# Start offsets within 128 bytes of the split weight and activation buffers in a hybrid decoder layer

## The reference, cut to what matters

```python
proj = h @ lp['w_in'] + lp['b_in']                       # D_MODEL 2048 -> 10288 columns
o_attn = attend(...) @ lp['w_attn_o']                    # 1024 -> 2048
o_rnn = (hs * jax.nn.gelu(r_y)) @ lp['w_rnn_o']          # 1024 -> 2048
out = (g_attn * o_attn + g_rnn * o_rnn) @ lp['w_out']    # 2048 -> 2048
...
gt, up = jnp.split((x * (1 + sc2) + sh2) @ lp['w_ffn_in'], 2, axis=-1)   # 2048 -> 2 x 5632
f = (jax.nn.silu(gt) * up) @ lp['w_ffn_out']             # 5632 -> 2048
```

## Time and profile before

| | |
|---|---|
| median of 3 runs | 1774.49 us (1772.01 to 1778.57) |
| the profiled execution | 1777.09 us |
| its span, first to last instruction | 1775.4 us |
| TensorE busy | 1737.5 us (98%) |
| weight loads | 1602.9 us (90%) |
| VectorE busy | 899.8 us (51%) |
| ScalarE busy | 711.3 us (40%) |
| mean granted TensorE clock | 0.99 of full speed |
| DMA | 216 GB/s on average |

### The profile page before, as it was taken

How to read it: one execution, slowest core, us unless ns; L and a number is a source line. 1 busy time by engine, 2 the same in 40 slices (tenths; PEclk the granted TensorE clock), 3 DMA queues, 4 the chain that set the end, 5 groups by cost and what they waited for, 6 DMA issues and landing times.

```text
span 1775.4 us, 34441 instructions
## 1 busy us (share of the span) xinstructions
PE 1737.5 (98%) x13514; PEld 1602.9 (90%) x13514; DVE 899.8 (51%) x1632; ACT 711.3 (40%) x1076; POOL 157.1 (9%) x271
## 2 busy tenths in 40 slices
PE   8989999999999999999999999999999999999997
PEld 3558879888999998889988899999999999999997
DVE  3233346655656655565873344444444444444565
ACT  2223227764545443343563333333333333333344
POOL 0001312213322311100000000000000000000001
PEclk9999999999999999999999999999999999999998
DMA  9998878766655647985647855545555454544552
GB/s 362 381 379 302 296 245 299 281 215 237 193 179 176 208 149 277 348 322 173 213 146 258 290 208 165 165 128 163 163 192 182 161 167 159 168 151 138 166 166 80
DMA packets 114151, 384.05 MB, mean 216 GB/s; under 512 B 14941, under 2 KB 15325, under 8 KB 113662
## 3 DMA queue, kind: packets, MB, share of 16 engines
q1 hardware_dynamic: 103248, 349.82, 57.1%
q0 software_dynamic: 10208, 32.32, 5.6%
q10 hardware_dynamic: 590, 0.44, 0.1%
HBM read 373.48 MB, written 9.03 MB: 215 GB/s over the span
## 4 chain that ended last, share of the span: by engine, by line
PE 90%; DMA 5%; DVE 2%; ACT 1%; SPq 1%; issue 1%; POOL 0%; POOLq 0%; ACTq 0%; DVEq 0%
PE bank L714 26%; PE bank L716 25%; PE bank L715 25%; DMA raw<-in_w_units 4%; PE bank L721 3%; PE bank L761 3%; PE bank L739 2%; PE bank L887 1%; SPq L478 1%; DVE wlo L377 1%; PE bank L1007 1%; PE bank L923 1%; DMA mgate<-mg 0%; ACT z L1510 0%; PE bank L954 0%
## 5 line engine op out<-in xcount | busy, mean ns | idle before, releaser
L714 PE MATMUL bank<-xhi,wlo 128*128 128x288 f32 x2544 | 759.2, 298 | 2.3 <-DVE wlo L377 1.7
L715 PE MATMUL bank<-xlo,whi 128*128 128x288 f32 x2544 | 751.0, 295 | 0.0
L716 PE MATMUL bank<-xhi,whi 128*128 128x288 f32 x2544 | 748.7, 294 | 0.0
L377 DVE TENSOR_TENSOR wlo<-raw,whi 128x1024 fp32r<-128x1024 f32 (+2 forms) x468 | 510.2, 1127 | 381.2 <-ACT whi L369 373.9
L369 ACT CAST whi<-raw 128x1024 fp32r<-128x1024 f32 (+2 forms) x468 | 434.6, 969 | 424.2 <-PE bank L716 273.8
L714 PEld LDWEIGHTS bank<-xhi,wlo 128*128 128x128 f32 x2544 | 477.5, 188 | 15.6 <-issue 13.7
L716 PEld LDWEIGHTS bank<-xhi,whi 128*128 128x128 f32 x2544 | 479.6, 189 | 0.0
L715 PEld LDWEIGHTS bank<-xlo,whi 128*128 128x128 f32 x2544 | 478.4, 188 | 0.6
L716 PE MATMUL bank<-hhi,whi 128*128 128x288 f32 x704 | 208.7, 296 | 0.0
L714 PE MATMUL bank<-hhi,wlo 128*128 128x288 f32 x704 | 208.3, 296 | 0.0
L715 PE MATMUL bank<-hlo,whi 128*128 128x288 f32 x704 | 205.2, 292 | 0.0
(11 more groups left out here) (332 smaller groups left out, 1674.9 us busy)
## 6 DMA issues: line engine op xcount, KB each, us to landing
raw<-in_w_units SPq DMA_DIRECT2D x556, 512.0 KB, 6.1
raw<-in_w_ffn_out_units SPq DMA_DIRECT2D x64, 384.0 KB, 3.1
raw<-in_w_ffn_out_units SPq DMA_DIRECT2D x64, 320.0 KB, 3.3
raw<-in_w_units SPq DMA_DIRECT2D x16, 448.0 KB, 8.6
mgate<-mg POOLq DMA_DIRECT2D x32, 144.0 KB, 4.3
mgl<-mgate POOLq DMA_DIRECT2D x16, 288.0 KB, 6.9
bz<-relrow POOLq DMA_DIRECT2D x16, 192.0 KB, 3.6
xt<-in_x SPq DMA_DIRECT2D x8, 288.0 KB, 7.4
```

The costliest lines, as they stand in the source:

```text
L377: nc.vector.tensor_tensor(wlo[e][:, part], raw[:, s, spot], f32(whi[e][:, part]), ALU.subtract).then_inc(raw_used[s][h], 1)
L714: pe.matmul(acc, wt[1][:, w], x[0][:, c, :], start=start, stop=False)
L715: pe.matmul(acc, wt[0][:, w], x[1][:, c, :], start=False, stop=False)
L716: return pe.matmul(acc, wt[0][:, w], x[0][:, c, :], start=False, stop=stop)
```

## The change

Ten buffers are allocated with some bytes of padding in front, and the view used by the program begins behind the padding. Nothing else is edited.

```diff
+        def behind(stack, name, pad, size):
+
+            return sbuf(stack, name, [P, pad // 4 + size], F32R)[:, pad // 4:]
+
+        def tokens(stack, name, pad, chunks):
+
+            return behind(stack, name, pad, chunks * T).rearrange("p (c t) -> p c t", t=T)
+
-        whi = [sbuf(ctx, f"whi{e}", [P, UNIT], F32R) for e in range(2)]
-        wlo = [sbuf(ctx, f"wlo{e}", [P, UNIT], F32R) for e in range(2)]
-        xhi = sbuf(ctx, "xhi", [P, DC, T], F32R)
-        xlo = sbuf(ctx, "xlo", [P, DC, T], F32R)
+        whi = [behind(ctx, f"whi{e}", (0, 64)[e], UNIT) for e in range(2)]
+        wlo = [behind(ctx, f"wlo{e}", (64, 32)[e], UNIT) for e in range(2)]
+        xhi = tokens(ctx, "xhi", 96, DC)
+        xlo = tokens(ctx, "xlo", 0, DC)
...
-        ohi = sbuf(p3, "ohi", [P, NP_, T], F32R)
-        olo = sbuf(p3, "olo", [P, NP_, T], F32R)
-        yhi = sbuf(p3, "yhi", [P, RC, T], F32R)
-        ylo = sbuf(p3, "ylo", [P, RC, T], F32R)
+        ohi = tokens(p3, "ohi", 64, NP_)
+        olo = tokens(p3, "olo", 0, NP_)
+        yhi = tokens(p3, "yhi", 16, RC)
+        ylo = tokens(p3, "ylo", 112, RC)
...
-        hhi = sbuf(hs, "hhi", [P, HALF, T], F32R)
-        hlo = sbuf(hs, "hlo", [P, HALF, T], F32R)
+        hhi = tokens(hs, "hhi", 48, HALF)
+        hlo = tokens(hs, "hlo", 112, HALF)
```

## The result

The median of 22 runs went from 1777.26 us to 1772.3 us. The ratio is 0.9973, with a 95% interval of 0.9964 to 0.9981. So the change makes the kernel faster by 0.27%, between 3.4 and 6.4 us, where 1.4 us slower had been forecast. It is less than the 0.5% that had been taken for what a measurement can tell, but 22 runs of each tell it.

A forecast was written before the change was run, and what follows sets the result against it. TensorE bounds the kernel: number of split-product matmuls times the distance of their starts. Terms -1.7 + 2.1 + 1.0 = +1.4 us on 1774.5 gave about 1776 us; forecast's own range 1770 to 1784, stated range 1758 to 1790.

The forecast's parts named there:

- (a): Even-numbered units with `xhi`, 79 of 159: offsets 0 against 0 as before, so no change in time.
- three points: Matmul spacing by streamed-minus-weight offset modulo 128: 133.3 ns at 0, 132.2 at 96, 134.2 at 32; straight lines between.
- d = 32: Streamed operand 32 bytes past the weights loaded beside it, modulo 128: 134.2 ns a matmul, from the `wx` units.
- (b): Odd-numbered units with `xhi`, 1280 blocks: new weight offsets give -1.3 ns a block, -1.7 us.
- (c): Units with `hhi`, 704 blocks, moved from 96 to 16: +1.6 us in even units, +0.5 us in odd.
- d = 16: Streamed operand 16 bytes past the weights loaded beside it, modulo 128: 133.75 ns by straight line, +1.55 ns for `hhi`.
- (d): The merge, 128 blocks with `ohi` at 32 and 128 with `yhi` at 48: together +1.0 us.
- (e): Mixed orders of L721, 3% of the chain: worth under 0.3 us, taken as 0.
- (f): The splits on ScalarE and VectorE: place within 128 bytes does nothing to them, and there is cover; 0.
- (g): VectorE's register instructions in the feed-forward input loops: 0, or 0.9 us with the cover gone.
- The faster one: Rival: offsets remove a good part of what the matmul steps lose; 1761 us at 2 ns per changed matmul; chance 0.24.
- The slower one: Rival: streamed operands starting off the 32-byte grid (`hhi`, `hlo`, `yhi`, `ylo`) cost time; 1788 us at 4 ns; chance 0.18.

## Why the prediction was wrong, point by point

**What bounds the kernel** was right: the time is the number of these matmuls times the distance of their starts, and nothing else moved. The reading of that distance from counts in stretches was good to 0.1 ns.

**(a) is the step that failed.** It put the even `xhi` units at "0 against 0, as before. Nothing", and they were worth -6.1 us, more than the whole result. It rested on the assumption that the difference of the places modulo 128 between the streamed operand and the weights loaded beside it decides. The run with only `wlo0` moved by 128 shows otherwise: places count modulo 256, and what acts first is the distance between the two weight buffers, 133.3 ns at 0 or 256, 132.4 at 64, 131.7 at 128. That the padding put 128 bytes between `whi0` and `wlo0` stands in the allocation, and could have been seen before the run; reducing it modulo 128 threw it away. Of the three points from which the other terms were drawn, the one for d = 32 fell too: its 134.2 ns became 133.3 when only the buffers of the unit ahead were moved.

**(b)** had -1.7 us and it was -1.6 (132.9 ns as forecast), but for another reason. The small offsets alone gave -0.7 us; the rest comes, by subtraction, with the further 128 bytes of `wlo1`.

**(c)** had +2.1 us and it was +1.9. Alone, with the weights of before, the move to 16 cost 0.6 ns and not the 1.5 of d = 16; the rest is the odd weights' doing. The agreement is partly luck.

**(d)** had +1.0 us and it was +0.2: 0.3 ns more for `ohi` and `yhi` alike, where the lines had up to 2.0.

**(e), (f) and (g)** were right: splits and register instructions cost nothing that shows.

**The rivals.** The faster one, that the offsets win back part of what a step loses, has the right sign and the wrong matmuls. The 6720 that were counted as changed lost 0.5 us together; the gain is that of the 3792 that were counted as untouched. Its reason against itself, that half of the `xhi` units aren't changed, was the failed step again. Of its reasons for itself, that even and odd units no longer start alike is out (both alike at 128 gave 131.7), and the 4 ns of L715 with `hlo` don't carry over to a block: in the `hhi` units before, the distance behind L715 is 129.0 ns, but those behind L714 and L716 are 134.9 and 133.1, and only their sum counts. The slower one, a penalty for starts off the 32-byte grid, is out at the size that it needed: `yhi` at 48 took 132.1 ns against 132.2, and `hhi` at 16 lost 0.6 ns where 3.6 was its threshold. The rule of the Trainium skill (TensorE: Matmul & The Clock Gate, Part 2) that loading weights takes nothing from the matmul that streams was read as no change for any layout. These runs have from 130.0 to 134.2 ns for a matmul of the same size and clock, and 133.3 against 131.7 with one buffer's address changed. So that conclusion doesn't hold for this stream of float32r matmuls with a weight load each; whether it is the weight load that disturbs the stream, no run shows.

**Open:** what in the chip makes the step depend on those distances, and what state a unit passes on. No run here looks inside a weight load. The three values from which the forecast drew its lines were means of a stream that can have more than one steady rhythm, and at least the one of `wx` depends on the unit ahead.

## What to carry to other kernels

In a kernel that is bound by back-to-back matmuls with a new weight load each, it can be worth trying the start addresses of the operands: here high and low weight buffers 128 bytes apart modulo 256 gave 0.5% for two lines of code, and no layout with several runs behind it gave more than 0.54%. When an offset is added, work out where everything behind it lands, and don't reduce to a smaller period than has been tested. And measure steps by the starts in the trace, since they repeat to 0.1 ns where whole runs scatter by several us.

## What the runs showed of the hardware that was not expected

The same matmul stream with the same buffers and the full granted clock ran at 130.0 ns in one place of an execution and at 132.2 in another. The choice was the same in two kernels in 85 of 90 units, and was passed on from unit to unit as a row of block times that repeats every two or every six blocks. With all four operands at the same place modulo 256 the average over a block was 133.3 ns, to about a tenth, whatever else was moved. And moving `xhi` and `xlo` together by 256 bytes changed nothing in the layout of before, while one low weight buffer moved by 128 took 1.6 ns off the matmuls of its units on average.
